# Moving 45 of 72 modulation slabs from the mixer to the two attention stages

## The reference, cut to what matters

```python
for l in range(2):
    ml = split(silu(c)     @ w_ada[l] + b_ada[l], 9)      # for the tokens
    mc = split(silu(c_ctx) @ w_ada[l] + b_ada[l], 9)      # for the context
    h  = h + 0.5 * ml[2] * swiglu(norm(h) * (1 + ml[1]) + ml[0])         # first half
    hn = norm(h) * (1 + ml[4]) + ml[3]
    h  = h + ml[5] * merge(attend_a(hn), attend_b(hn), fourier(hn))      # attention
    h  = h + 0.5 * ml[8] * swiglu(norm(h) * (1 + ml[7]) + ml[6])         # second half
```

## Time and profile before

| | |
|---|---|
| median of three runs | 3096.66 us (3096.48 to 3105.07) |
| span of the profiled execution | 3098.7 us |
| PE busy in it | 2918.9 us, 94% |
| mean granted clock of PE | 0.967 of full speed |
| DVE, ACT, POOL busy | 49%, 33%, 11% |

### The profile page before, as it was taken

One profiled execution on the slowest core, in us unless ns is written; L12 is line 12 of the kernel. 1 busy time (PEld: TensorE's weight loads), 2 busy tenths in 40 slices (PEclk: granted clock), 3 DMA queues, 4 the chain that ended last, 5 costly groups with the idle time before them and its releaser, 6 DMA issues.

```text
span 3098.7 us, 55748 instructions
## 1 busy us (share of the span) xinstructions
PE 2918.9 (94%) x24053; PEld 2390.2 (77%) x24053; DVE 1508.6 (49%) x2228; ACT 1010.2 (33%) x1468; POOL 337.0 (11%) x405
## 2 busy tenths in 40 slices
PE   6988897899999899999899999999999998989999
PEld 6876675677777689876578878888788887769999
DVE  6534323233333266672763444445544456386666
ACT  3211213222222244532642332222322225264543
POOL 5122100000000000142100010000100004310000
PEclk9998898999999999999999999999999999999999
DMA  6346669999999945311012222222222222104552
GB/s 251 123 165 259 269 263 400 421 393 390 392 386 387 369 151 190 132 60 41 1 55 95 109 109 95 95 95 95 82 95 95 95 95 82 55 14 177 219 190 82
DMA packets 77071, 547.89 MB, mean 177 GB/s; under 512 B 8384, under 2 KB 10432, under 8 KB 11056
## 3 DMA queue, kind: packets, MB, share of 16 engines
q1 hardware_dynamic: 76000, 540.05, 44.8%
q0 software_dynamic: 848, 4.57, 0.4%
HBM read 637.91 MB, written 1.05 MB: 206 GB/s over the span
## 4 chain that ended last, share of the span: by engine, by line
PE 86%; DVE 7%; DMA 3%; ACT 2%; POOL 1%; issue 1%; DVEq 0%; POOLq 0%; SPq 0%; ACTq 0%
PE bank L778 56%; PE bank L1155 11%; PE bank L1505 2%; DMA ring<-slabs 2%; PE bank L842 1%; DVE tiny L2777 1%; PE bank L1357 1%; PE bank L970 1%; PE bank L957 1%; PE bank L1361 1%; PE bank L1364 1%; PE bank L1674 1%; PE bank L1682 1%; PE bank L1593 1%; PE bank L1678 1%
## 5 line engine op out<-in xcount | busy, mean ns | idle before, releaser
L778 PE MATMUL bank<-hhi,whi 128*128 128x256 f32 (+1 forms) x1280 | 431.2, 337 | 0.6 <-ACT wk L2018 0.4
L778 PE MATMUL bank<-hlo,whi 128*128 128x256 f32 (+1 forms) x1280 | 430.4, 336 | 0.0
L778 PE MATMUL bank<-hhi,wlo 128*128 128x256 f32 (+1 forms) x1280 | 429.2, 335 | 0.0
L2200 DVE TENSOR_TENSOR wlo<-ring,whi 128x2048 fp32r<-128x2048 f32 x132 | 298.9, 2287 | 205.8 <-ACT whi L1706 200.2
L778 PE MATMUL bank<-fhl,whi 128*128 128x256 f32 (+1 forms) x1408 | 343.8, 335 | 0.0
L1706 ACT ACTIVATE whi<-ring 128x2048 fp32r<-128x2048 f32 x132 | 252.3, 1913 | 210.0 <-PE bank L778 209.9
L1155 PE MATMUL bank<-ring,wk 128*32 128x256 f32 x4064 | 251.9, 391 | 21.1 <-DMA ring<-slabs 15.7
L778 PEld LDWEIGHTS bank<-fhl,whi 128*128 128x128 f32 x1408 | 240.0, 188 | 31.4
L778 PEld LDWEIGHTS bank<-hhi,whi 128*128 128x128 f32 x1280 | 240.5, 188 | 29.8 <-issue 1.7
L778 PEld LDWEIGHTS bank<-hlo,whi 128*128 128x128 f32 x1280 | 241.1, 188 | 26.8
L778 PEld LDWEIGHTS bank<-hhi,wlo 128*128 128x128 f32 x1280 | 240.3, 188 | 26.2
(11 more groups left out here) (497 smaller groups left out, 5573.5 us busy)
## 6 DMA issues: line engine op xcount, KB each, us to landing
ring<-slabs SPq DMA_DIRECT2D x542, 1024.0 KB
wk<-slabs SPq DMA_DIRECT2D x45, 1024.0 KB, 12.6
ac<-slabs SPq DMA_DIRECT2D x16, 1024.0 KB, 12.5
wk<-mixp POOLq DMA_DIRECT2D x1, 1040.0 KB, 12.1
xt<-xT SPq DMA_DIRECT2D x1, 1024.0 KB, 6.7
xt<-ctxT POOLq DMA_DIRECT2D x1, 1024.0 KB, 12.0
out<-xt SPq DMA_DIRECT2D x4, 256.0 KB, 2.4
cst<-maskc POOLq DMA_DIRECT2D x1, 960.0 KB, 14.6
```

The source lines that it names most:

```text
L778: last = pe.matmul(o, a, b, start=k == 0, stop=k == len(pairs) - 1)
L2200: tt_(wlo_of(n), slab(n), whi_of(rel).bitcast(F32), ALU.subtract).then_inc(sem("wlo"), 1)
```

## The change

27 slabs stay in the first block: 1 before each inverse, 12, 7 (was 10) and 4. The 24 inside the inverses, `ADA_GMAT`, the 6 ahead of the output projection and the 8 behind the second norm are gone from there. 29 slabs move into the attention stage of layer 0 and 16 into that of layer 1: one behind each Fourier unit, then 2 and 1 by turns behind `turns_of(n)` of the first 14 (layer 0) or 8 (layer 1) jobs. They are new numbers of the ring, behind the eleven slabs of the projection and ahead of those of the merge.

For that, the coded vectors are made anew by POOL in each layer (`CSIL2`), the column selector again by DVE (`SEL32B`), all late products use bank 7, `values` uses bank 6 alone and so waits for the result just before, ACT's copies of a full bank, PE's turns and DVE's additions stand at set steps (`ROW_AT`, `TURN_AT`), the splits of the first gate and branch slab move from steps 4 and 6 to 18 and 20 (layer 0) and 9 and 11 (layer 1), and `scales` of the second half stands behind the jobs.

```diff
-N_LATE = 8
+N_MIX = 27
+ADA_L = (29, 16)
...
+def lay(l, x):
+    return S_LAYER + N_LAYER * l + sum(ADA_L[:l]) + x + (ADA_L[l] if x >= L_MERGE else 0)
...
-ADA_PREP, ADA_MAT, ADA_GLA, ADA_GMAT, ADA_NORM = 12, 1, 10, 4, 4
+ADA_PREP, ADA_MAT, ADA_GLA, ADA_NORM = 12, 1, 7, 4
+ADA_SETS = ((0, 16), (16, 11), (27, 16), (43, 13), (56, 16))
+ROW_AT = ({5: 2, 14: 3}, {8: 4})
+TURN_AT = ({6: 2, 15: 3}, {9: 4})
+GATE_SPLIT, BRANCH_SPLIT = (18, 9), (20, 11)
+def att_ada(l, n):
+    return 2 - n % 2 if n < (14, 8)[l] else 0
...
@@ POOL, in the projection @@
+                    if i == 7:
+                        pool.wait_ge(sem("silc"), 1)
+                        pool.wait_ge(sem("vt"), 10 * l + 2)
+                        pool.memset(CSIL2[:, :, 0:30], 0.0)
+                        pool.memset(CSIL2[:, :, 32:62], 0.0)
+                        pool.tensor_copy(CSIL2[:, :, 30:32], ...).then_inc(sem("csz"), 1)
@@ PE @@
+            def ada_product(n, b, coded):
+                ...
+                for k in range(KT):
+                    strip = slice(32 * (k % 4), 32 * (k % 4) + 32)
+                    mm = pe.matmul(bank[b][strip, 0:FB], coded[:, k, 30 - 2 * i:62 - 2 * i], s[:, k, :],
+                                   start=i == 0 and k < 4, stop=last and k >= 4)
+                ...
+            def late_ada(l, k):
+                for _ in range(k):
+                    n = ada_n[0]
+                    if n == N_MIX + sum(ADA_L[:l]):
+                        pe.wait_ge(sem("csz"), 2 + l)
+                    for g, (first, _) in enumerate(ADA_SETS):
+                        if n == first:
+                            pe.wait_ge(sem("adr"), g)
+                    slab_wait(pe, ada_slab(n))
+                    ada_product(n, 7, CSIL2)
+                    ada_n[0] += 1
@@ PE, each level of an inverse @@
-                        if lv:
-                            ada(1)
@@ PE, gated linear attention; ahead of the output projection; behind the second norm @@
-            ada(ADA_GMAT)
...
-            ada(N_ADA - N_LATE - ada_n[0])
+            ada_t(1, 7, SEL32)
...
-            ada(N_LATE)
@@ PE, Fourier units and jobs @@
                     if n:
                         four2(n - 1)
+                    late_ada(l, 1)
...
                 def values(n):
-                    if n >= 2:
-                        pe.wait_ge(sem("pvc"), j0 + n - 1)
+                    if n:
+                        pe.wait_ge(sem("pvc"), j0 + n)
+                    if n + 1 in TURN_AT[l]:
+                        ada_t(TURN_AT[l][n + 1], 6, SEL32B)
...
                     turns_of(n)
+                    late_ada(l, att_ada(l, n))
@@ ACT, jobs @@
-                    if n == 4:
+                    if n in ROW_AT[l]:
+                        ada_row(ROW_AT[l][n], 7)
+                    if n == GATE_SPLIT[l]:
                         split_att(l, att_gate(0))
-                    if n == 6:
+                    if n == BRANCH_SPLIT[l]:
                         split_branch(l, 0)
@@ DVE, jobs @@
                     dve.wait_ge(sem("pv"), j0 + n + 1)
+                    if n + 1 in TURN_AT[l]:
+                        ada_mods(TURN_AT[l][n + 1], 6)
...
                 result(len(js) - 1)
+                dve.wait_ge(sem("modc"), (4, 5)[l])
+                scales(5 + 3 * l)
```

More of the change, by code:

```diff
@@ L59 @@
 N_ADA = 2 * NMOD * D // FB
-N_LATE = 8
[L61 to L67, removed]
+N_MIX = 27
+ADA_L = (29, 16)
+S_WOUT = S_ADA + N_MIX
+S_MOE = S_ADA + N_MIX + 4
 CAP = 32
@@ L95, with ada_slab @@
 N_LAYER = L_FFN1 + 3 * B_FFN
-NSLABS = S_LAYER + 2 * N_LAYER
+def lay(l, x):
+    return S_LAYER + N_LAYER * l + sum(ADA_L[:l]) + x + (ADA_L[l] if x >= L_MERGE else 0)
+NSLABS = lay(1, N_LAYER)
+def ada_slab(n):
+    if n < N_MIX:
+        return S_ADA + n
+    l = int(n >= N_MIX + ADA_L[0])
+    return lay(l, L_MERGE - 1) + 1 + n - N_MIX - sum(ADA_L[:l])
 def added(n):
@@ L109 @@
 V_BRANCH = [merge_half(h) + 3 for h in range(6)]
-VIRTUAL = sorted(V_BRANCH + [V_SRC, V_OUT, V_OUT + 1])
+VIRTUAL = {lay(l, v) for l in range(2) for v in V_BRANCH + [V_SRC, V_OUT, V_OUT + 1]}
 DRAM_LAYER = S_MOE + N_EXP
@@ L115, with dram @@
 D_LAYER = D_FFN1 + 3 * B_FFN
-N_DRAM = DRAM_LAYER + 2 * D_LAYER
+def dram(l, x):
+    return DRAM_LAYER + D_LAYER * l + sum(ADA_L[:l]) + x + (ADA_L[l] if x >= D_MERGE else 0)
+N_DRAM = dram(1, D_LAYER)
 N_ATT = 33
@@ L435, in slot @@
             s = (n - S_LAYER + SKEW) % NSLOT
-            before = [m for m in range(S_LAYER, n) if (m - n) % NSLOT == 0 and (m - S_LAYER) % N_LAYER not in VIRTUAL]
+            before = [m for m in range(S_LAYER, n) if (m - n) % NSLOT == 0 and m not in VIRTUAL]
             return s, S_MOE // NSLOT + N_MOE // (NSLOT + NXTRA) + (s < SKEW) + len(before)
@@ L835, in ada @@
                     slab_wait(pe, ada_slab(n))
[L836 to L851, removed]
+                    ada_product(n, 6 + n // ADA_G, CSIL)
+                    if n == ADA_G + ADA_TURN - 1:
+                        ada_t(0, 6, SEL32)
+                    ada_n[0] += 1
[9 more added lines that the diff above has]
+                    ada_product(n, 7, CSIL2)
                     ada_n[0] += 1
@@ L2245, in norm @@
                         ins.then_inc(sem("hl"), 1)
-                    if n < 8:
+                    if n < 8 and k != 1:
                         scales(n + 1)
@@ L2958, in _slabs @@
         l, c = divmod(n, N_ADA // 2)
-        out[ada_slab(n)] = _cols(g["w_ada_2"][l], c * FB, FB)
+        with_l = int(n >= N_MIX + ADA_L[0])
+        at = S_ADA + n if n < N_MIX else dram(with_l, D_MERGE - 1) + 1 + n - N_MIX - sum(ADA_L[:with_l])
+        out[at] = _cols(g["w_ada_2"][l], c * FB, FB)
     for n in range(4):
@@ L3002, in _slabs @@
         for n in range(4):
-            out[s + D_WOUT + n] = _cols(g["w_out_2"][l], n * FB, FB)
+            out[dram(l, D_WOUT + n)] = _cols(g["w_out_2"][l], n * FB, FB)
     return out
```

126 lines of the change are left out of this document (65 added, 61 removed).

## The result

The changed kernel takes 3128.8 us, the median of 4 runs (3127.6 to 3136.0), against 3096.6 us for the kernel before on the same chip: 32.2 us slower, a ratio of 1.0111 with a 95% interval of 1.0097 to 1.0126. The prediction said slower by 15.9 us, 3112.6. The sign was right, the size half of what came.

A forecast was written before the change was run, and what follows sets the result against it. PE was taken as the bound, with 86% of the chain, and DVE in the second half of the jobs. Savings of 26.5 us against 42.4 added gave 15.9 us slower, 3112.6 us, range 3092 to 3132.

The forecast's parts named there:

- 1 inverses: Four inverses without their 24 slabs: levels shorten by up to 0.72 us each, 16.5 us saved, bounds 10 and 24.4.
- 2 `ADA_GMAT`: Four slabs and a turn removed at `ADA_GMAT`, DVE then next: 3.2 us saved, bounds 3 and 4.3.
- 3 ahead of the output projection: Six slabs removed before the output projection, PE then waits for `mixr`: 4.3 us saved, bounds 4 and 7.4.
- 4 behind the second norm: Eight slabs removed behind the second norm: 2.5 us saved; bounds -1 and 8.2, router products possibly slower at lower clock.
- 5 experts' stretch: Expert loads start earlier, but the ring is full when the experts begin, before as after: 0 gained.
- 6 Fourier units: Twelve slabs added in the Fourier units, where PE has no gap: 12.0 us lost, bounds 10.9 and 13.
- 7 and 8 first halves: Slabs in first attention jobs: layer 1 loses 11.6 us; layer 0 loses 13.8 of 20.8, gaps hiding 7.
- 9 splits: Splits in the second halves, where DVE is the bound, slow it beside POOL: 5 us lost, bounds 0 and 10.
- 10 waits and small work: Attention stages: `values` waiting for the previous result, slab landing and small POOL and ACT work cost 0.
- I had this as a rival: Clock falls in the inverses: twenty levels without slabs stay low, losing 1.4 us each, 28 us: 3141; chance 0.10.
- the gaps: Rival: PE's idle time in attention jobs fills, only 17.5 of 44.4 us shows: 3087.7 us; chance 0.12.
- the full worth of every product: Rival: every removed product was worth its full time, 44.3 us saved against 42.4 added: 3095; chance 0.16.

The follow-up runs named there:

- e5: Kernel before with values of every job in bank 6 alone, waiting for the result of the job ahead: 3099.9 us against 3095.2 (1.0012).
- e1: Changed kernel with eight idle matmuls put back into each of levels 1 to 6 of the four inverses: 3132.2 us against 3097.5 for the kernel before (1.0115).
- e2: Changed kernel with eight idle matmuls in levels 5 and 6 only of each inverse: 3120.7 us against 3097.5 for the kernel before (1.0068).
- v2: Kernel before with one group of eight idle matmuls behind the masks' products and one in level 0 of each inverse: 3090.6 us against 3095.9 (0.9984).
- v4: Kernel before with idle groups behind the masks' products, in level 0 and behind the first product after each inverse: 3088.4 us against 3097.6 (0.9976).
- e4: Kernel before with only the splits moved, to jobs 18 and 20 (layer 0), 9 and 11 (layer 1): 3106.8 us against 3095.2 (1.0035).
- e6: Changed kernel with 42 of the 45 products in the attention stages left out: 3091.6 us against 3095.2 for the kernel before (0.9995).
- e0: Kernel before, unchanged, profiled once more: span 3097.9 us.
- e10: Kernel before with one matmul of eight left in each of 22 products in the inverses: 3098.1 us against 3097.6 (0.9997).
- e7: Kernel before with 22 of the 24 products in the inverses left out, slabs still loaded: 3117.1 us against 3095.9 (1.0075).
- v3: Kernel before with one group of eight idle matmuls behind the first product after each inverse: 3092.9 us (0.9994).
- e8: Changed kernel with the splits in jobs 11 and 13 (layer 0), 5 and 7 (layer 1): 3120.9 us against 3095.9 for the kernel before (1.0082).

## Where the prediction failed, and where it held

| item | forecast | measured in the trace |
|---|---|---|
| 1 inverses | -16.5 | -18.2, and +11.1 between and behind them |
| 2 `ADA_GMAT` | -3.2 | -3.1 |
| 3 ahead of the output projection | -4.3 | -3.9, and +2.0 in it |
| 4 behind the second norm | -2.5 | -2.2, and +2.9 in the router |
| 5 experts' stretch | 0 | -6.6 |
| 6 Fourier units | +12.0 | +14.2 |
| 7 and 8 first halves | +25.4 | +22.0 |
| 9 splits | +5 | +13.1 |
| 10 waits and small work | 0 | 0 for the one bank (e5), the rest not measured alone |
| start, and norms and blocks between the stages | 0 | -4.2 |
| sum | +15.9 | +27.1 |

- **The failed step is the clock in items 1, 3 and 4.** The sum put the clock at nothing. The removed time itself was right: 27.4 us for 26.5. But from the inverses to the router only 11.4 of it came back, since 16.0 us went to the 1.2 GHz level behind the places that the products had left (11.1, 2.0 and 2.9). I had this as a rival, with the wrong place: I asked whether the levels of the inverses would slow, found their new gap small, and gave it 0.10. The later levels did not slow: they are 3.50 us apart. What slowed was the next stretch, which runs small matmuls with waits of 0.6 to 0.8 us between them. With the products ahead of it, it had run at 1.00 or 0.81; with idle matmuls in their place it does so again (e1, e2). For item 4 I named the lower clock and the price (up to 3.8) and left it out of the sum; it was +2.9. The rule that I quoted (the Trainium skill, TensorE: Matmul & The Clock Gate, The HAM clock gate) says that the throttled state is the default and activity releases it; that filler may then pay for itself was my inference. The runs agree: e2, v2 and v4 added filler and were 8.0, 5.3 and 9.2 us faster than the kernels without it.
- **Item 9 was the second mis-sized term**, outside its bound of 10. I priced DVE's three scalings at 1.0 us a job. Beside POOL its smallest scaling and product slow as well, 0.17 to 0.59 and 0.16 to 0.57 (e4). DVE is 5.1 us longer busy in each second half, and in layer 0 PE, waiting, fell to the lower level for some of the jobs (clock 0.85 for 0.93). What the splits gave back at their old place, 3.2 and 1.2 us in e4, did not show in the changed kernel. In e6, with hardly a product there, the first halves are only 0.5 and 0.0 us below before's as well, so the products are not the whole reason; it was not tested further.
- **Item 6** was 2.2 short, beyond its bound: the slab costs 1.00 and the eight products beside it 0.15 more; over the twelve slabs it came to 1.18 each. That is on the side of the drain at a change of tiling (the Trainium skill, TensorEngine Tiling (Array Packing), Key Properties), though no run tells the drain from other causes; I had set 0.09 for it.
- **Items 2, 3, 7 and 8** held (3 apart from the clock, a tenth under its lower bound), and so did item 10 as far as it was tested, but that in layer 1 the eight jobs grew by 9.3, under my lower bound of 10: of twelve slabs, one of the two in the first job and the one in the last cost nothing. In layer 0 the gaps took 8.1 of 20.8, where I let 7 vanish.
- **Item 5** missed a gain. The experts' DMA waits are 22.5, 22.9 and 16.1 us for 25.5, 23.2 and 18.3:

```profile
511.06 22.54 DMA ring<-slabs
545.38 22.91 DMA ring<-slabs
1003.41 16.13 DMA ring<-slabs
```

  But the stretch varies as much where the change is absent. In the profiles of before's code with all 72 slabs loaded it takes 605.1, 604.1, 601.8 and 601.8 us (before, e0, e4, e5), 605.9 in e10, 596.5 in e7, and 599.6, 600.8 and 600.1 in v2, v3 and v4; with the changed kernel's loads it takes 595.6 to 601.9. Fewer loads ahead of the experts may help, but e7 and v2 to v4 have much of the gain without that. The cause stays open, and the 6.6 us may in good part belong to the executions.

- **The -4.2** lies in work that the change does not touch. 2.7 of it stands between the jobs of layer 0 and the Fourier units of layer 1, where the clock is low at two places for longer in before than in the changed kernel (at the second 0.79 over 2190 to 2198 us, against 1.00 over 2202 to 2208). In e8, the same code there, that part takes 1135.3 us as in before (1135.2), against 1132.5: chance of the execution.
- **The base.** I took the median as 2.0 below the span; a run is 1.8 above its own span. The profiled execution of before lay 3.9 us above its median, that of after 1.1 below. So of the 16.3 us by which the forecast missed in the medians, 11.2 are the terms of the table and the rest is this.

The rivals in which the gaps or the full worth of every product decide are refuted: the first by the 14.2 us of the Fourier units and the 22.0 of the first halves, the second by levels 3.50 us apart.

## What to carry to other kernels

Before taking filler-like work out of a stage, look at the granted clock not only there but in the next stretch: if that stretch waits often, price it at the lower level, or leave idle matmuls in the last steps ahead of it. Move elementwise work of the other engines to where PE is the bound, never to where DVE is: in the changed kernel the same splits cost 13 us in one half of a stage and 2 us in the other (e8). And when a part is left out for a test, see that its signals still come at the old pace.

## What the runs showed of the hardware

- The stretch behind an inverse has the same instructions in every variant (DVE 5.99 us) and takes 15.4 us at clock 1.00, 18.2 at 0.81, 19.3 at 0.73 and 19.5 at 0.74. PE counts as busy for 84% to 87% of it in all four, so that the busy share alone does not show the loss.
- With the loads of before and one matmul left of eight (e10), the stretch behind the first inverse had 0.81; it had 1.00 with all of them and 0.74 with none in the changed kernel.
- One matmul left of a group of eight takes 0.55 us of PE's chain (e10), all eight 1.00.
- POOL at work stretches some of DVE's instructions and not others (e4): a scaling of two columns 3.5 times (0.17 to 0.59), a product of one column 3.6 times (0.16 to 0.57), a scaling of 128x256 2.9 times in the chain (0.28 to 0.82), a reciprocal of two columns not at all (0.15 and 0.16).
